# Window attention of a fused transformer kernel: the scores of each head as two fp32r products over 128 rows in place of one fp32 product over 64

## What is computed

```
qkv = h @ w_qkv + b_qkv
q = qkv[..., :1024].reshape(B, S, 2, 8, 64) * 64 ** -0.5
k = qkv[..., 1024:1152].reshape(B, S, 2, 64)
v = qkv[..., 1152:].reshape(B, S, 2, 64)
# per block of 128 queries, over the 256 keys of its own block and the one before
s = einsum('bqhgd,bshd->bhgqs', qn, kn) + bias
s = where(mask, s, NEG_INF)
m = maximum(max(s), sink); e = exp(s - m); p = e / (sum(e) + exp(sink - m))
out = einsum('bhgqs,bshd->bqhgd', p, vn)
```

## Time and profile before

| | |
|---|---|
| median of 3 executions | 1934.51 us (1933.03 to 1934.76) |
| the profiled execution | 1933.36 us, of which span 1931.5 us |
| instructions in the trace | 25271 |
| TensorE (PE) busy | 1908.9 us, 99% |
| VectorE (DVE), ScalarE (ACT), GpSimd (POOL) busy | 55%, 40%, 18% |
| `a_kv` and `a_q` on TensorE | about 756 to 807 us |
| window attention | about 807 to 871 us |

### The profile page before, as it was taken

The page is one execution under the profiler, slowest core; times in us unless marked ns, Lnnn a source line. Parts: engine busy times, 40 slices in busy tenths (PEclk is TensorE's granted clock), DMA queues, the critical chain, the costliest instruction groups (busy, mean ns, idle before and its releaser), DMA issues.

```text
span 1931.5 us, 25271 instructions
## 1 busy us (share of the span) xinstructions
PE 1908.9 (99%) x9688; PEld 1505.7 (78%) x9688; DVE 1056.6 (55%) x2005; ACT 769.1 (40%) x1407; POOL 354.1 (18%) x443
## 2 busy tenths in 40 slices
PE   9999999999999999999999999999999999999998
PEld 7887778888777668768888888888766788888886
DVE  5576644444699765475544443343777555444323
ACT  4343434433454554474322222232566442222213
POOL 0640000001130761062000000040266310000002
PEclk9999999999999999999999999999999999999999
DMA  9452324443413223313333333365100133333332
GB/s 208 133 173 68 104 90 148 147 142 82 110 62 93 71 56 88 93 50 92 96 98 98 98 93 101 91 185 169 34 2 2 46 97 98 101 96 99 99 98 77
DMA packets 297246, 187.67 MB, mean 97 GB/s; under 512 B 32543, under 2 KB 274719, under 8 KB 296870
## 3 DMA queue, kind: packets, MB, share of 16 engines
q1 hardware_dynamic: 288958, 168.02, 30.8%
q10 hardware_dynamic: 8168, 18.03, 2.5%
HBM read 183.79 MB, written 17.96 MB: 104 GB/s over the span
## 4 chain that ended last, share of the span: by engine, by line
PE 90%; DVE 6%; ACT 2%; issue 1%; DMA 1%; POOL 0%; ACTq 0%; SPq 0%; DVEq 0%
PE banks L298 21%; PE banks L300 21%; PE banks L299 21%; PE banks L2031 4%; PE banks L2000 4%; PE banks L2014 4%; PE banks L600 2%; PE banks L599 2%; PE banks L598 2%; PE banks L412 2%; PE banks L414 2%; PE banks L413 2%; PE banks L950 1%; DVE idx_score L1216 1%; PE banks L958 1%
## 5 line engine op out<-in xcount | busy, mean ns | idle before, releaser
L2397 DVE TENSOR_TENSOR wlo<-raw,whi 128x1024 fp32r<-128x1024 f32 (+1 forms) x281 | 361.5, 1288 | 323.7 <-ACT whi L2388 323.2
L298 PE MATMUL banks<-xs,wlo 128*128 128x512 f32 x1336 | 531.9, 398 | 0.1
L300 PE MATMUL banks<-xs,whi 128*128 128x512 f32 x1336 | 520.6, 390 | 0.0
L299 PE MATMUL banks<-xs,whi 128*128 128x512 f32 x1336 | 520.3, 389 | 0.0
L2388 ACT ACTIVATE whi<-raw 128x1024 fp32r<-128x1024 f32 (+1 forms) x281 | 293.1, 1045 | 249.7 <-PE banks L300 100.1
L298 PEld LDWEIGHTS banks<-xs,wlo 128*128 128x128 f32 x1336 | 250.8, 188 | 60.6 <-issue 7.5
L299 PEld LDWEIGHTS banks<-xs,whi 128*128 128x128 f32 x1336 | 251.0, 188 | 54.2 <-issue 3.4
L300 PEld LDWEIGHTS banks<-xs,whi 128*128 128x128 f32 x1336 | 250.7, 188 | 52.8
L524 POOL TENSOR_TENSOR squares<-squares,x_tmp 128x512 f32<-128x512 f32 x35 | 46.9, 1341 | 685.3 <-ACT x_tmp L516 685.3
L2126 POOL TENSOR_SCALAR prob<-prob,long_stat,gt_s 128x512 f32<-128x512 f32 (+3 forms) x128 | 77.1, 612 | 124.6 <-DVE long_stat L2074 124.6
L2961 ACT ACTIVATE a_hi<-ff_tmp 128x512 fp32r<-128x512 f32 x44 | 27.8, 632 | 166.1 <-DVE ff_tmp L2960 166.1
(11 more groups left out here) (402 smaller groups left out, 3216.9 us busy)
## 6 DMA issues: line engine op xcount, KB each, us to landing
raw<-in_ffn_w_gu SPq DMA_DIRECT2D x88, 512.0 KB, 3.8
raw<-in_e_w_in SPq DMA_DIRECT2D x56, 512.0 KB, 3.9
raw<-in_ffn_w_down SPq DMA_DIRECT2D x38, 512.0 KB, 3.5
s_skew<-s_bias ACTq DMA_DIRECT2D x6, 2560.0 KB
raw<-in_o_w_in SPq DMA_DIRECT2D x21, 512.0 KB, 4.0
raw<-in_e_w_out SPq DMA_DIRECT2D x16, 512.0 KB, 3.9
raw<-in_b_w_in SPq DMA_DIRECT2D x15, 512.0 KB, 3.9
raw<-in_a_w_qkv SPq DMA_DIRECT2D x10, 512.0 KB, 4.0
```

Of the source, the lines that this page charges most:

```text
L298: nc.tensor.matmul(out, k.wlo[:, chunk.slot, at, :], self.x_hi(kt), start=first, stop=False)
L299: nc.tensor.matmul(out, k.whi[:, chunk.slot, at, :], self.x_lo(kt), start=False, stop=False)
L300: ins = nc.tensor.matmul(out, k.whi[:, chunk.slot, at, :], self.x_hi(kt), start=False, stop=last)
L2397: self.nc.vector.tensor_tensor(self.wlo[:, chunk.slot, 0:chunk.blocks, :], self.raw[:, chunk.slot, 0:chunk.blocks, :], hi.bitcast(F32), AL ...
```

## The change

Each head's query is kept as a high part (rounded to fp32r) and a low part (the rest), above each other in 128 rows of `q_both`; for head 0 the high part lies in rows 0 to 63, for head 1 in rows 64 to 127, and the low part in the other half. The keys are kept as high and low, each in both row halves. The score of a head is the product of these 128 rows with the low keys plus that with the high keys. Products are never narrower than 256 columns. The key tile gets four more steps, on VectorE, and every query tile two ScalarE steps and two more VectorE steps, each on 64x512. The trailing tile's added VectorE steps stand at s = 4. `win_lo` no longer shares the place of the queries.

```diff
-    def evict(self, eng, who, n):
+    def evict(self, eng, who, n, some=range(99)):
...
-            if engine != who:
+            if engine != who or i not in some:
                 continue
...
             for x in range(2):
+                if self.key_low is not None:
+                    both, n = self.q[:, 2 * m + x, t * P:(t + 1) * P], max(nk, 2 * P)
+                    nc.tensor.matmul(S(s, x)[:, 0:n], both, self.key_low(e, m)[:, k0:k0 + n], start=True, stop=False)
+                    ins = nc.tensor.matmul(S(s, x)[:, 0:n], both, self.key(e, m, x)[:, k0:k0 + n], start=False, stop=True)
+                    continue
...
             if self.trail and s == 2:
-                self.before.evict(dve, "dve", self.before.tiles - 1)
+                self.before.evict(dve, "dve", self.before.tiles - 1, range(2))
+            if self.trail and s == 4:
+                self.before.evict(dve, "dve", self.before.tiles - 1, range(2, 99))
...
-            q_at = self.line_up()
-            qT = self.sb(c, "qT_w", [P, MT, 512])
-            kT = self.sb(c, "kT_w", [P, 2, 512])
+            self.line_up()
+            o_lo = self.sb(c, "win_lo", [P, MT, 512], F32R)
+            k_hi = self.sb(c, "k_hi_w", [P, 2, 512], F32R)
+            k_lo = self.sb(c, "k_lo_w", [P, 2, 512], F32R)
...
-            o_lo = self.place("win_lo", [P, MT, 512], F32R, q_at)
+            q_both = self.sb(c, "q_both_w", [P, NH, 512], F32R)
 
             def q_steps(n):
                 t = tmp[:, n % 2, :]
+
+                def high(x):
+                    r = slice(64 * x, 64 * x + 64)
+                    return ("act", lambda ps: nc.scalar.activation(q_both[r, 2 * n + x, :], t[r, :], ACT.Identity, bias=bqs[r, n:n + 1]))
+
+                def low(x):
+                    r, other = slice(64 * x, 64 * x + 64), slice(64 - 64 * x, 128 - 64 * x)
+                    return ("dve", lambda ps: nc.vector.scalar_tensor_tensor(q_both[other, 2 * n + x, :], t[r, :], bqs[r, n:n + 1],
+                                                                             q_both[r, 2 * n + x, :].bitcast(F32), ALU.add, ALU.subtract))
                 return [("dve", lambda ps: nc.vector.scalar_tensor_tensor(t, ps, -HD ** -0.5, rb, ALU.mult, ALU.mult)),
-                        ("act", lambda ps: nc.scalar.activation(qT[:, n, :], t, ACT.Identity, bias=bqs[:, n:n + 1]))]
+                        high(0), high(1), low(0), low(1)]
...
-                    return ("act", lambda ps: nc.scalar.activation(kT[64 * to:64 * to + 64, g, :], t[r, :], ACT.Identity,
+                    return ("act", lambda ps: nc.scalar.activation(k_hi[64 * to:64 * to + 64, g, :], t[r, :], ACT.Identity,
                                                                    bias=bk[r, :]))
-                return scaled + [part(g, to) for g in range(2) for to in range(2)]
+
+                def low(g, to):
+                    r = slice(64 * g, 64 * g + 64)
+                    return ("dve", lambda ps: nc.vector.scalar_tensor_tensor(k_lo[64 * to:64 * to + 64, g, :], t[r, :], bk[r, :],
+                                                                             k_hi[r, g, :].bitcast(F32), ALU.add, ALU.subtract))
+                both = [(g, to) for g in range(2) for to in range(2)]
+                return scaled + [part(g, to) for g, to in both] + [low(g, to) for g, to in both]
```

More of the change, by code:

```diff
@@ L1913, in __init__ @@
                  mask=None, sink=None, gate=None, branches=1, bias_all=None, masked_bias=None, ready=None, finishing=None,
-                 mask_made=None, turning=None, first_pe=None, first_act=None, trail_act=None, first_dve=None):
+                 mask_made=None, turning=None, first_pe=None, first_act=None, trail_act=None, first_dve=None, key_low=None):
         self.k, self.q, self.key, self.value, self.keys, self.n_bias = k, q, key, value, keys, n_bias
@@ L1922, in __init__ @@
         self.turning, self.first_pe, self.first_act, self.following = turning, first_pe, first_act, None
-        self.first_dve = first_dve
+        self.first_dve, self.key_low = first_dve, key_low
         self.pad = 0 if sink is None else 1
@@ L2937, in windowed @@
             attention = Attention(
-                self, qT, lambda e, m, x: kT[:, m // 4, :],
+                self, q_both, lambda e, m, x: k_hi[:, m // 4, :],
                 lambda e, m, x, b, r: vt[0:r, b, (m // 4) * HD:(m // 4 + 1) * HD], keys, 256, lambda m: self.oT[:, m, :],
-                lambda m: o_hi[:, m, :], lambda m: o_lo[:, m, :], self.in_streams(1, stat, [early[:, 0:1026], early[:, 1026:1540]]), before=a_q, trail_act=2, table=1, bias=bias, sink=sink,
+                lambda m: o_hi[:, m, :], lambda m: o_lo[:, m, :], self.in_streams(1, stat, [early[:, 0:1026], early[:, 1026:1540]]), key_low=lambda e, m: k_lo[:, m // 4, :], before=a_q, trail_act=2, table=1, bias=bias, sink=sink,
                 ready=lambda pe, m, e: pe.wait_ge(self.sig("tile_steps").sem, a_q.done(m)))
```

## The result

| | before | after |
|---|---|---|
| median, 8 executions of each | 1933.90 us (1932.88 to 1935.20) | 1939.72 us (1939.51 to 1940.97) |
| profiled execution, its span | 1933.36, 1931.5 us | 1939.79, 1938.0 us |

The ratio is 1.0032, with a 95% interval of 1.0023 to 1.0041. The time lies in the predicted range (1933.8 to 1941.7). The outcome called likeliest, a change within 0.2%, was missed: the loss is 5.8 us where 3.25 were forecast. The two profiled executions are 6.43 us apart. One execution of a later variant (e1: 3173.79 us at a mean clock of 0.555) is left out of all that follows.

A forecast was written before the change was run, and what follows sets the result against it. TensorE, busy for 99% of the span, was taken to bound the kernel. The terms 2.05 + 1.7 - 0.5 gave +3.25 us, on the median of 1934.51 us a forecast of 1937.8 us, range 1933.8 to 1941.7.

The forecast's parts named there:

- The key tile's low parts: In `a_kv`, four added VectorE instructions delay the next weights' low part, so TensorE waits 2.05 us more.
- the rival that had 0.04: Clock falls to 1.2 GHz in a longer wait, about 773 us: +3 us, +6 in all, 1940.5 us; chance 0.04.
- The start of attention: While attention's pipeline fills, the trailing tile's added copies and low parts delay turn(2) by 0.95, turn(4) by about 1.7 us.
- The scores: In attention's steady cycle, 256-column fp32r products spaced 0.12 us, groups of 0.59; about -0.08 us a cycle, -0.5 in all.
- The rival of expensive narrow products: In attention, narrow score products not at half price: 1948 us at 0.23 each, 1941 at 0.16; chance 0.13.
- TensorE's gain taken back by VectorE: In attention's cycle, TensorE alone gains 0.19 us; VectorE takes most back, leaving about 0.08 a cycle.
- the rival of the shorter cycle: In attention, TensorE's shorter cycle arrives whole and the fill absorbs its part: about +0.3, 1934.8 us; chance 0.16.
- the mix's wait: In attention's cycle, VectorE's links release the mix 0.13 us earlier; with an equally late start, at best 0.05.
- The forecast's own bounds: Two stalls, 1.75 to 2.25 and 0.95 to 2.4 us, cycle hardly moving: +1.5 to +5.5 us; chance 0.61.

The follow-up runs named there:

- e1: Changed kernel, in `a_kv` the second query tile's weights split ahead of the key tile's copies and low parts: 1936.69 us, ratio 1.0017.
- e12: Kernel before plus the trailing tile's two VectorE low parts at step 4 and a second ScalarE copy at step 2, into spare tile: 1935.95 us, ratio 1.0013.
- e11: Kernel before plus only two VectorE low parts of the trailing query tile at step 4, into a spare tile: 1934.82 us, ratio 1.0007.
- e6: Changed kernel with block 0's score products 128 columns wide in place of 256: 1939.09 us, ratio 1.0026.
- e2: Changed kernel with the trailing tile's second copies moved to steps 10 and 14, its low parts to 16 and 20: 1939.66 us, ratio 1.0034.
- e5: Kernel before plus four VectorE low parts of 64x512 behind the key tile's copies, into an unread tile: 1936.98 us, ratio 1.0018.
- e8: Changed kernel with one extra VectorE copy of 128x2 per attention step, into an unread tile: 1940.5 us, ratio 1.0038.
- e3: Changed kernel with early split of weights in `a_kv` and the trailing tile's copies and low parts moved to later steps: 1937.16 us, ratio 1.0020.
- e9: Kernel before with one extra VectorE copy of 128x2 per attention step, into an unread tile: 1934.46 us, ratio 1.0005.

## Why the prediction was right, and where it was short

*The key tile's low parts*: right. The forecast was 2.05 us behind four instructions of 0.78; the runs show 2.03 to 2.04 behind four of 0.77. That 64 rows save nothing was right too.

*The clock*: the rival that had 0.04 is what happened, in part. The forecast cited 1.00 with TensorE idle for 0.98 us and took that as cover for a wait twice as long. It was none: the clock fell behind 2.03 us, and seven of the eight executions of the changed kernel lie within 0.4 us of each other. The price is half of what the rival said, 1.62 us against 3: the stretches show 3 x 0.41 + 3 x 0.16 = 1.7 us of clock missing, while the rival doubled 3 us of products. This is the first failed step: a term left out of the sum. The Trainium skill ("TensorE: Matmul & The Clock Gate", "Why this matters for your kernels") advises against idle gaps between bursts of products only where they are longer than any wait here. This trace differs: a gap of 2.03 us was enough.

*The start of attention*: the mechanism was right and the size was not, 3.29 us against 1.7. Turn(2) had 0.95 and got 1.76. ScalarE's second copy gives 0.76 of that, shown alone in e12. Of the remaining 1.00, 0.88 is `logit(2)`, which the forecast had moving by 0.2: it starts 819.11 - 817.34 = 1.77 us behind `score(2)` in place of 0.89. VectorE's queue is 1.65 us late against TensorE, not 1.3 (1.37 by its own chain, and TensorE is 0.28 sooner), so `share(1)` at 818.60 holds `logit(2)` by 0.54, and a pause of 0.26 comes on top. Then the forecast let turn(4) be 0.7 us less late than `keep(1)`. That is the second failed step: with the low parts alone (e11) `keep(1)` was 1.56 and turn(4) 1.31 us late, so 0.25 are absorbed. It is 0.26 with all four steps and the clock at 1.00 (e1: 3.35 and 3.09), and next to nothing in the changed kernel, whose products behind the wait run at the lower clock (3.32 and 3.29).

*The scores*: right. Spacing 0.12 as forecast, first product 0.10 more (forecast 0.11), group 0.58 (0.59), turn 0.53, cycle 6.53 (6.4 to 6.6), gain 0.35 (0.5). The rival of expensive narrow products is refuted by e6 as well, down to 128 columns.

*TensorE's gain taken back by VectorE*: the mechanism is shown by the two kernels with a spare copy. The reason given against the rival of the shorter cycle, the mix's wait, was the right one to weigh against 1.0 us of idle time.

*Additivity*: the key tile's low parts alone cost +0.18%, the fill alone +0.13%; together that is 0.31%, against 0.32% for the whole change. This includes whatever the clock did in each, and each figure is good to 0.1% only, so that they agree so closely is chance.

*The range*: that the time lies in it is in part luck. The forecast's own bounds (+1.5 to +5.5 us) end at 1940.0; the range went on to 1941.7 without a term for it. The loss, 5.8 us by the medians and 6.3 by the traces, is beyond these bounds, by the clock, which had no term, and by the fill, 3.29 us where its upper bound was 2.4. And the forecast started from 1934.51 us, the median of three executions of which two were of the slower group of that kernel; from 1933.4 its sum would have given 1936.7, 3.0 us short of the time in place of 1.9.

What stays open: why a wait, of 0.7 us or of 2 us, is followed by the lower clock in one execution and not in the next. The Trainium skill (the same page, "What's actually happening") says of the warm-up that its point of change varies from run to run of one kernel. For the fall, the groups of times of one program point the same way; no run here shows what decides it. The pause of 0.26 us ahead of `logit(2)` stands while GpSimd divides (817.88 to 819.79 in the trace after); that it is the cause was not tried.

## What to carry to other kernels

Cost a new wait of a busy TensorE twice: its own length, and the clock behind it, here 1.6 us for a wait of 2 us with TensorE setting the pace (and nothing in the end behind the changed kernel's second wait, where VectorE set it), in some executions or in all. Before a scatter is put down to the change, look whether the kernel before has it too, and where in its trace the clock is low. An engine's idle time in a cycle is not its slack: 1.0 us idle was 0.14 us of slack, and a tiny extra instruction on the suspected engine measures it, by the cycle in the trace rather than by the median. When delays are moved onto a chain that runs through several engines, add them up until a row shows an engine that waits for nothing in that chain.

## What the hardware did that was not expected

**VectorE and GpSimd slow each other down** when VectorE reads two tensors: beside two low parts, GpSimd's two divisions of 128x128 take 1.71 us in place of 0.72 (818.43 in the kernel before), in the changed kernel, in e11 and in e12 (those 0.72 stand beside a VectorE copy that reads one tensor, the `keep` at 818.26); and a low part of 0.77 us takes 1.14 to 1.23 beside GpSimd's work in e2. The Trainium skill ("GPSIMD Engine Reference", Specifications) states that the two share SBUF interfaces, with contention where VectorE has two SBUF inputs; these rows agree.

**Narrow fp32r products**: 512 columns 0.227 us apart, 256 columns 0.12, 128 columns 0.11, all with their weight loads hidden. Going from 256 to 128 columns gains 0.01 us a product.

**The clock at half rate under a fully busy TensorE**: 8 or 9 products counted in 3 us in place of 15 behind a wait of 2.03 or 2.04 us, with the fp32 scores (e5) as with the new ones; and not always behind the same wait (e8).

**The clock falls behind short waits too**: of 1.16 us in e3 (0.71 from 840 to 843 us), and of 0.70 us at the start of e9 (0.84 and 0.74 from 24 to 32 us).
